# The retention gate's in-projection as pairs of tiles in seven block products, with its token sums made during the value projection

## The chip, the cores and the metric

The kernel runs on one core of one Trainium2 chip. The metric is device time in microseconds. Beside the timed runs there is one profiled execution, from which all rows below come. TensorE (PE) does the matrix products, VectorE (DVE) and ScalarE (ACT) the elementwise work, GpSimd (POOL) and SyncE (SP) mostly issue DMAs, each on a queue of its own that issues in program order.

## The reference

A two-layer decoder trunk on 1024 tokens of width 1024: a retention layer with an MLP, then an attention layer with an MLP, each sub-layer behind an RMS norm with shift and scale from a conditioning vector c. The part in question is the retention layer's in-projection:

```python
def retention_mixer(h, positions, w_in, norm_gain, w_out, gammas):
    proj = h @ w_in                                   # (1024, 1024) @ (1024, 6144)
    q, k, v, g = jnp.split(proj, [qk_w, 2 * qk_w, 2 * qk_w + v_w], axis=-1)
    q, k = rotary(q, positions), rotary(k, positions)
    y = rms_norm(retention(q, k, v, gammas), norm_gain)
    return (jax.nn.silu(g) * y) @ w_out               # g: 2048 columns

ada = c_act @ w_ada[layer] + b_ada[layer]             # shift, scale, gate of each sub-layer
```

The products are in f32. The kernel splits each operand in a high part (rounded) and a low part (the rest) and adds three products, high x high, high x low and low x high.

## The kernel before

Everything is held with features on the partitions and tokens in the free dimension. `h_hi` and `h_lo` hold the normed input (8 tiles of 128 features by 1024 tokens), `xT` the residual stream. Weights come in pairs of tiles: SP loads 256 columns (1 MB) into a slot of `w_raw` (`load_pair`), ACT rounds them into `w_hi` (`prep`, L916), VectorE makes `w_lo` (L1361), TensorE uses them. There are two slots, and SP's next load into one waits for `lo_done`.

The retention in-projection has three stages, each four trips of two pairs: q and k (with rotary), v (tokens as output rows, `v_unit`, L2209 to L2213), and the gate g (`in_body` and `in_unit`, L2077 to L2083). In the gate stage each unit is one tile of 128 columns for 1024 tokens: 8 steps of k, two halves of the tokens, three products, 48 matmuls of 128x512. ACT applies silu while it evacuates (`evac`, L966), POOL spills the tile to `g_s` in DRAM (`spill`, L714).

Beside these stages the modulation is made: for every chunk of 1024 columns of `w_ada` (or `kv_w_ada`) SP loads 8 tiles of 512 KB into two buffers `ada_raw` in turn (`ada_load`, L544), VectorE multiplies each by c and adds it up (`ada_tile`, L1374 and L1377), TensorE sums over the partitions (`ada_sums`, 16 small matmuls, L2153) and VectorE adds the bias (`ada_columns`, L1385). SP's `body` issues one load of weights and then four of the modulation, again and again, and each modulation load waits for the tile two before it. In the gate stage these tiles are all that VectorE does beside `w_lo`.

The first MLP's in-projection already uses seven block products: per pair of tiles, `in_products` (L2420 to L2422) computes seven products of 12 matmuls into three banks. Its weight sums (`in_sums`, L1736 to L1741), splits (`in_low`, L1746) and adds (`add_c22` at L1753 and others) are VectorE's, the copies out of the banks (`keep`) ACT's. Before the seventh product TensorE waits for `add_c22`, which has to read the bank first. No modulation tiles are made in that stage.

After the gate stage the first retention head starts (`ret_head(0)`) on q, k and v that POOL loads back: the first halves (`rq_first`, `rk_first`, `rv_first`) during the gate stage, the rest behind it.

Of the kernel before, what the change touches and what calls it, by code (L numbers as in the profile page):

```python
# [21 lines left out]
ALU = mybir.AluOpType  # L22
# [22 lines left out]
W_QK, W_V, W_G = 0, 8, 16  # L45
W_RET = 24
W_MLP0 = 32
W_FK, W_FV = 36, 40
W_FQ, W_OG = 44, 48
W_FOX = 52  # L50
W_MLP1 = 56


A_QK, A_V, A_G, A_MLP0 = 8, 24, 56, 72
A_FK, A_FF, A_FV, A_FQ, A_OG, A_MLP1, A_OUT = 76, 84, 85, 101, 109, 117, 121
# [10 lines left out]
E_QK, E_V, E_G, E_FK, E_FV, E_FQ, E_OG = 16, 80, 80, 144, 176, 176, 208  # L66
T_V, T_FK, T_FV, T_FQ = 16, 144, 144, 208
# [30 lines left out]
def build(nc, x, vec_a, vec_b, forget_bias, positions, w_ada, kv_w_ada, w_mlp_in, w_mlp_out, ret_w_in,  # L98
          ret_w_out, kv_w, fox_w_in, fox_w_out, ret_decay, out):
    with ExitStack() as ctx:  # L100
# [6 lines left out]
        def region(nbytes, *layouts):  # L107

            base, sets = nc.sbuf_base, []
            for layout in layouts:  # L110
# [23 lines left out]
            _, rq_first, rk_first, rv_first), (_, sq_low) = region(  # L134
# [5 lines left out]
            [("above_ret", [P, 4, S], F32), ("rq_first", [P, 2, HALF], F32), ("rk_first", [P, 2, HALF], F32),  # L140
             ("rv_first", [P, 4, RET_DV], F32)],
# [60 lines left out]
        ada_ps, ada_ps_v = bank[6], bank[0]  # L202
# [101 lines left out]
        z_last_loaded = sem("z_last_loaded")  # L304
        x_moved = [sem(f"x_moved{i}") for i in range(4)]
# [126 lines left out]
        NQ = 14  # L432

# [17 lines left out]
        def in_batch(q, b):  # L451

            raw = (lambda: raw_part(q, 0, 0, 8), lambda: sum_rows(0, 2), lambda: sum_rows(2, 2),
                   lambda: raw_part(q, 1, 4, 4))[b]()
            first, count, n = ((0, 2, P), (2, 2, HALF), (4, 2, HALF), (6, 1, P))[b]
            return raw, split_part(w_hi, first, count, n), split_part(w_lo, first, count, n)
# [11 lines left out]
        def in_operand(i):  # L468
# [4 lines left out]
            return t_tiles({2: 1, 3: 0, 4: 2, 6: 3}[i])[1:]  # L473
# [4 lines left out]
        def t_split(layer, i, order=FIRST_LO):  # L478

            return layer * 4 * (NQ + 1) + order.index(("t", i)) + 1  # L480

        def in_split(layer, q, b, order=FIRST_LO):

            return layer * 4 * (NQ + 1) + (order.index(("w", b)) + 1 if q == 0 else 4 * q + b + 5)

        def t_summed(layer, n):

            return layer * (4 * NQ + 13) + n

        def in_summed(layer, q, n):  # L490

            return layer * (4 * NQ + 13) + 13 + 4 * q + n

        def in_banks(q):

            return (bank[4], bank[5], bank[6]) if q % 2 == 0 else (bank[0], bank[1], bank[2])

# [21 lines left out]
        def _(sp):  # L519
# [46 lines left out]
            with sp.Fori(0, 3) as i:  # L566
                body(i * 2 + W_QK, [in_pair(ret_w_in, i * 512 + 512 + 256 * j) for j in range(2)],
                     i + 2, w_ada[0], i * 1024 + 2048)
            body(W_V - 2, [half_pair(ret_w_in, j, 2048) for j in range(2)], 5, w_ada[0], 5120)
# [3 lines left out]
            for i, (w_a, col_a) in enumerate([(w_ada[1], 3072), (w_ada[1], 4096), (w_ada[1], 5120), (kv_w_ada, 0)]):  # L573
                body(i * 2 + W_G - 2, [in_pair(ret_w_in, i * 512 + 4096 + 256 * j) for j in range(2)],
                     i + 9, w_a, col_a)
            body(W_G + 6, [out_pair(ret_w_out, 0, j) for j in range(2)], 13, kv_w_ada, 1024)
# [4 lines left out]
            def mlp_loads(base, layer, d_end):  # L581
                for j in range(2):
                    load_pair(base + j, j, in_pair(w_mlp_in[layer], 256 * j))

                def x_quarter(hf, kh):
                    return x_s[4 * kh:4 * kh + 4, :, half(hf)].rearrange("k p n -> p k n")
# [5 lines left out]
                def load_in(q):  # L592
                    if q < 2:
                        sp.wait_ge(lo_done, base + q + 1)
                    else:
                        sp.wait_ge(split_lo_done, in_split(layer, q - 2, 3))
# [24 lines left out]
                sp.wait_ge(split_lo_done, in_split(layer, NQ - 2, 3))  # L621
                load_a(0, A11, (0,))
                sp.wait_ge(split_lo_done, in_split(layer, NQ - 1, 2))
                reload_x(1, 1)
                sp.wait_ge(split_lo_done, in_split(layer, NQ - 1, 3))
                load_a(0, A11, (1,))
                sp.wait_ge(in_full, layer * 7 * NQ + 7 * NQ)
# [61 lines left out]
        def _(pool):  # L689
# [52 lines left out]
            for j in range(4):  # L742
                pool.wait_ge(stage_dma[j], E_G)
            for j in range(2):
                pool.wait_ge(stage_dma[T_SLOT + j], T_FK)

# [10 lines left out]
            for dst, src in ((rk_first[:], qk_s[8:10, :, 0:HALF].rearrange("a p n -> p a n")),  # L757
                             (rq_first[:], qk_s[0:2, :, 0:HALF].rearrange("a p n -> p a n")),
                             (rv_first[:], v_s[0:HALF, 0:RET_DV].rearrange("(b p) n -> p b n", p=P))):
                pool.dma_start(dst, src).then_inc(ret_first_loaded, 16)  # L760
            with pool.Fori(0, 4) as i:
                for j in range(4):
                    spill(j, g_s[bass.ds(i * 4 + j, 1)].rearrange("a p n -> p (a n)"),
                          a_free, i * 4 + (A_G + j + 1))
            pool.wait_ge(a_full, A_MLP0)
# [22 lines left out]
            for j in range(4):  # L788
                pool.wait_ge(stage_dma[j], E_FK)
# [116 lines left out]
        def _(act):  # L906
# [104 lines left out]
            def v_trip(i, w_base, a_base, t_base, stage_free, order, after=None):  # L1011

                prep(i * 2 + (w_base + 1), 1)
                prep(i * 2 + (w_base + 2), 0)
# [8 lines left out]
            with act.Fori(0, 4) as i:  # L1023
# [1664 lines left out]
```

## Time and profile before

| | us |
|---|---|
| median of 3 runs | 2971.44 (2969.31 to 2971.76) |
| profiled execution | 2969.84 |
| its span | 2968.2 |
| PE busy | 2926.6 (99%) |
| DVE busy | 1716.2 (58%) |
| ACT busy | 1018.2 (34%) |
| DMA, mean | 145 GB/s |

All times in rows count from the span's start. A matmul is listed with 389 ns, but matmuls are pipelined, so their pitch is read from the starts. PEclk is the granted TensorE clock as a share of 2.4 GHz.

### The profile page before, as it was taken

To read this page: it belongs to the slowest core of one execution; us is meant where nothing else is said; L and a number is where in the kernel's file an instruction comes from. 1 tells how busy PE (TensorE), PEld (TensorE's weight loads), DVE (VectorE), ACT (ScalarE), POOL (GpSimd) and SP (SyncE) were. 2 spreads that over 40 slices of the span, in tenths; PEclk is the share of its full clock that TensorE was granted. 3 is DMA by queue.
4 is the path that set the end of the run, shared out by engine and by line. 5 is a ranking of instruction groups with operands and counts; after the bars stand their busy time and mean duration, and the time that the engine had idled before them with its cause. 6 is when DMAs were issued, how large, how long until landed. Compare 5 with 4: busy or idle time off the path is not lost.

```text
span 2968.2 us, 33444 instructions
## 1 busy us (share of the span) xinstructions
PE 2926.6 (99%) x13020; PEld 2353.8 (79%) x13020; DVE 1716.2 (58%) x2106; ACT 1018.2 (34%) x1287; POOL 339.3 (11%) x486
## 2 busy tenths in 40 slices
PE   7999999999999999999999999999999999999999
PEld 5788888877777888888888787876766888888887
DVE  6664323345457977676756344245455787768673
ACT  5111122233224433334335435334244433333331
POOL 1000010010002000111111001122120200011110
PEclk8999999999999999999999999999999999999999
DMA  6565555542232444565412323455342344475431
GB/s 235 182 208 186 203 192 194 198 169 65 88 118 71 159 144 155 194 233 179 151 35 89 131 79 123 160 131 119 87 105 72 114 160 151 147 261 192 135 135 57
DMA packets 182630, 431.01 MB, mean 145 GB/s; under 512 B 12849, under 2 KB 74724, under 8 KB 182500
## 3 DMA queue, kind: packets, MB, share of 16 engines
q0 software_dynamic: 61616, 222.34, 22.5%
q1 hardware_dynamic: 120884, 206.88, 20.9%
q8 instruction: 88, 1.44, 0.2%
q14 instruction: 42, 0.34, 0.0%
HBM read 309.90 MB, written 119.14 MB: 145 GB/s over the span
## 4 chain that ended last, share of the span: by engine, by line
PE 91%; DVE 4%; ACT 2%; DMA 1%; issue 1%; POOL 0%; SPq 0%; DVEq 0%; ACTq 0%; POOLq 0%
PE ps L2442 6%; PE ps L2422 6%; PE ps L2444 6%; PE ps L2421 6%; PE ps L2420 6%; PE ps L2440 6%; PE ps L2077 5%; PE ps L2083 5%; PE ps L2080 5%; PE ps L2121 4%; PE ps L2120 4%; PE ps L2117 4%; PE ps L2572 3%; PE ps L2209 3%; PE ps L2213 3%; PE ps L2212 3%
## 5 line engine op out<-in xcount | busy, mean ns | idle before, releaser
L2440 PE MATMUL ps<-z_hi,w_hi 128*128 128x512 f32 x768 | 299.0, 389 | 0.0
L2444 PE MATMUL ps<-z_hi,w_lo 128*128 128x512 f32 x768 | 299.0, 389 | 0.0
L2442 PE MATMUL ps<-z_lo,w_hi 128*128 128x512 f32 x768 | 299.0, 389 | 0.0
L2077 PE MATMUL ps<-h_hi,w_hi 128*128 128x512 f32 x704 | 275.8, 392 | 2.7 <-DVE w_lo L1361 2.2
L2080 PE MATMUL ps<-h_lo,w_hi 128*128 128x512 f32 x704 | 274.6, 390 | 0.0
L1361 DVE TENSOR_TENSOR w_lo<-w_raw,w_hi 128x2048 fp32r<-128x2048 f32 x60 | 137.4, 2290 | 149.8 <-ACT w_hi L916 149.8
L2083 PE MATMUL ps<-h_hi,w_lo 128*128 128x512 f32 x704 | 217.7, 391 | 0.0
L2117 PE MATMUL ps<-z_hi,w_hi 128*128 128x512 f32 x512 | 203.6, 398 | 0.0
L2121 PE MATMUL ps<-z_hi,w_lo 128*128 128x512 f32 x512 | 199.6, 390 | 0.0
L2120 PE MATMUL ps<-z_lo,w_hi 128*128 128x512 f32 x512 | 199.5, 390 | 0.0
L916 ACT ACTIVATE w_hi<-w_raw 128x2048 fp32r<-128x2048 f32 x60 | 114.6, 1910 | 221.5 <-PE ps L2209 116.7
L1377 DVE SCALAR_TENSOR_TENSOR misc<-misc,c_act 128x1024 f32<-128x1024 f32 x84 | 107.9, 1284 | 125.8 <-DMA misc<-w_ada 105.9
L1530 DVE SCALAR_TENSOR_TENSOR xT<-ps,ada,xT 128x512 f32<-128x512 f32 x128 | 93.9, 748 | 147.5 <-PE ps L2121 147.5
L966 ACT ACTIVATE stage<-ps 128x1024 f32<-128x1024 f32 x56 | 57.4, 1026 | 344.8 <-PE ps L2083 274.8
L2422 PE MATMUL ps<-h_hi,w_lo 128*128 128x512 f32 x448 | 174.4, 389 | 0.0
L2421 PE MATMUL ps<-h_lo,w_hi 128*128 128x512 f32 x448 | 174.4, 389 | 0.0
L2420 PE MATMUL ps<-h_hi,w_hi 128*128 128x512 f32 x448 | 174.4, 389 | 0.0
L2440 PEld LDWEIGHTS ps<-z_hi,w_hi 128*128 128x128 f32 x768 | 144.2, 188 | 29.9
L2442 PEld LDWEIGHTS ps<-z_lo,w_hi 128*128 128x128 f32 x768 | 144.2, 188 | 29.8
L2444 PEld LDWEIGHTS ps<-z_hi,w_lo 128*128 128x128 f32 x768 | 144.2, 188 | 29.8
L2077 PEld LDWEIGHTS ps<-h_hi,w_hi 128*128 128x128 f32 x704 | 132.7, 188 | 31.0 <-DVE w_lo L1361 3.5
L2083 PEld LDWEIGHTS ps<-h_hi,w_lo 128*128 128x128 f32 x704 | 132.6, 188 | 27.7
(345 smaller groups left out, 6360.6 us busy)
## 6 DMA issues: line engine op xcount, KB each, us to landing
t_s<-misc POOLq DMA_DIRECT2D x28, 1792.0 KB, 6.9
misc<-t_s POOLq DMA_DIRECT2D x98, 512.0 KB, 4.1
misc<-w_ada SPq DMA_DIRECT2D x80, 512.0 KB, 5.1
w_raw<-w_mlp_in SPq DMA_DIRECT2D x32, 1024.0 KB, 5.5
w_raw<-ret_w_in SPq DMA_DIRECT2D x24, 1024.0 KB, 7.7
a_bufs<-w_mlp_out SPq DMA_DIRECT2D x12, 1024.0 KB, 22.7
a_bufs<-w_mlp_out SPq DMA_DIRECT2D x12, 768.0 KB, 6.0
qk_s<-stage POOLq DMA_DIRECT2D x16, 512.0 KB, 4.0
```

The costliest lines, as they stand in the source:

```text
L2077: m = MM(outs[hf], hi, b_hi[:, k, cols], start=first, stop=False)
L2080: MM(outs[hf], hi, b_lo[:, k, cols], start=False, stop=False)
L2083: m = MM(outs[hf], lo, b_hi[:, k, cols], start=False, stop=last)
L2117: mm = MM(out_bank, hi, z_hi[:, k, half(hf)], start=k == 0, stop=False)
L2120: MM(out_bank, hi, z_lo[:, k, half(hf)], start=False, stop=False)
L2121: mm = MM(out_bank, lo, z_hi[:, k, half(hf)], start=False, stop=k == 3)
L2420: MM(out, hi, b_hi[:, k, :], start=k == 0 and i in (0, 1, 3), stop=False, skip_group_check=True)
L2421: MM(out, hi, b_lo[:, k, :], start=False, stop=False, skip_group_check=True)
L2422: mm = MM(out, lo, b_hi[:, k, :], start=False, stop=k == 3, skip_group_check=True)
L2440: MM(bank[at + m], hi, ring_b(z_hi, slot)[:, cols], start=first and i not in (2, 4, 5), stop=False, skip_group_check=True)
L2442: MM(bank[at + m], hi, ring_b(z_lo, slot)[:, cols], start=False, stop=False, skip_group_check=True)
L2444: mm = MM(bank[at + m], lo, ring_b(z_hi, slot)[:, cols], start=False, stop=last, skip_group_check=True)
```

## The change

The gate stage uses the seven products too, for 8 pairs of tiles, 84 matmuls a pair in place of 96. The former function inside the MLP becomes one for three phases (`ph` 0 is the gate, 1 and 2 the MLPs), with counters offset by the pairs before. What is added, and where:

- SP spills the four quarters of `xT` to scratch behind the last q/k loads, and loads them back when the last pair's adds are done. In between `xT` holds four sums of the tokens' blocks.
- VectorE makes these sums (`gate_t_sums`, ten operations of 128x2048) behind the modulation tiles of the first three value trips; ACT and VectorE split them before and after the fourth. The order of VectorE's work in the gate stage is written out by hand, below.
- SP loads a gate pair into `w_raw` when the pair two before it has been split, and four modulation tiles behind it.
- ACT copies three partial products a pair, applies silu to the finished tiles in place, and loads silu's table once. POOL spills two tiles a pair, from two slots instead of four.
- The first loads for retention move behind the seventh pair's spills and wait for products of the eighth pair.

```diff
 # SP
+            for n in range(4):
+                sp.dma_start(x_quarter(n // 2, n % 2), xT[quarter(n // 2, n % 2)]).then_inc(x_moved[n], 16)
+            def load_gate(q):
+                if q < 2:
+                    sp.wait_ge(lo_done, W_V + 7 + q)
+                else:
+                    sp.wait_ge(split_lo_done, in_split(0, q - 2, 3))
+                sp.dma_start(dst, in_pair(ret_w_in, 4096 + 256 * q)).then_inc(in_loaded[q % 2], 16)
+            for i, (w_a, col_a) in enumerate([... five chunks, the first is chunk 9 ...]):
+                for j in range(2):
+                    if i < 4:
+                        load_gate(2 * i + j)
+                    else:
+                        sp.wait_ge(split_lo_done, in_split(0, NG - 2 + j, 3))
+                        load_pair(W_RET + j, j, out_pair(ret_w_out, 0, j), first=True)
+                    for k in range(4 * j, 4 * j + 4):
+                        ada_load(i + 9, k, w_a, col_a)
+            sp.wait_ge(c_added, added(0, NG - 1, 3))
+            for n in range(4):
+                sp.dma_start(xT[quarter(n // 2, n % 2)], x_quarter(n // 2, n % 2)).then_inc(x_moved[n], 16)
 # ACT
+            for q in range(NG):
+                if q:
+                    gate_out(q - 1)          # silu of the fourth tile, out of the bank
+                    gate_high(q, 3)          # waits for the seventh product of q - 1
+                    gate_silu(q - 1)         # in place, two operations; POOL spills after them
+                gate_keep(q, 0)
+                if q + 1 < NG:
+                    gate_high(q + 1, 0)
+                gate_keep(q, 1)
+                gate_keep(q, 2)
+                if q + 1 < NG:
+                    gate_high(q + 1, 1)
+                    gate_high(q + 1, 2)
 # VectorE
+            def gate_low(q, b):
+                raw, hi, lo = in_batch(q, b, gate_sum_rows)
+                dve.wait_ge(split_hi_done, in_split(0, q, b))
+                TT(lo, raw, hi.bitcast(F32), ALU.subtract).then_inc(split_lo_done, 1)
+            v_trip(3)
+            gate_sums(0)
+            gate_t_low(2)
+            gate_t_low(1)
+            gate_low(0, 0)
+            gate_low(0, 1)
+            ada_columns(9, ada_ps_v)
+            gate_low(0, 2)
+            gate_t_low(3)
+            gate_low(0, 3)
+            for q in range(NG):
+                chunk = 10 + q // 2
+                if q:
+                    gate_low(q, 3)
+                    if q % 2 == 0:
+                        ada_columns(chunk - 1, ada_ps_g)
+                for k in range(4 * (q % 2), 4 * (q % 2) + 2):
+                    ada_tile(chunk, k)
+                if q + 1 < NG:
+                    gate_sums(q + 1)
+                    gate_low(q + 1, 0)
+                for k in range(4 * (q % 2) + 2, 4 * (q % 2) + 4):
+                    ada_tile(chunk, k)
+                if q + 1 < NG:
+                    gate_low(q + 1, 1)
+                for n in range(3):
+                    gate_add(q, n)
+                if q + 1 < NG:
+                    gate_low(q + 1, 2)
+                else:
+                    prep(W_RET, 0)
+            ada_columns(13, ada_ps_g)
 # TensorE
+            for q in range(NG):
+                in_products(0, q, ((A_V + 25, A_V + 26, A_V + 27), (A_MLP0, 0, 0)), gate_t_tiles, gate_banks)
+                if q % 2:
+                    ada_sums(10 + q // 2, ada_ps=ada_ps_g)
 # inside in_products, as in the MLP before
                 for i in range(7):
                     if i in (0, 2, 4, 6):
+                        pe.wait_ge(split_lo_done, in_split(ph, q, i // 2))
                     if i == 6:
+                        pe.wait_ge(c_added, added(ph, q, 1))
```

## Rows read from the trace of the kernel before

**Rows 1.** The page: busy time of TensorE, and the chain that ended last.
```profile
PE 2926.6 (99%) x13020; PEld 2353.8 (79%) x13020; DVE 1716.2 (58%) x2106; ACT 1018.2 (34%) x1287; POOL 339.3 (11%) x486
...
PE 91%; DVE 4%; ACT 2%; DMA 1%; issue 1%; POOL 0%; SPq 0%; DVEq 0%; ACTq 0%; POOLq 0%
```

**Rows 2.** Windows (busy us per engine, PEclk, DMA share, GB/s): value, gate, MLP in-products.
```profile
242.10:423.70 181.60, 181.59 (x832) 151.47 (x833) 64.01 (x50) 33.44 (x39) 11.79 (x17) 1.00 0.55 188
423.70:605.20 181.50, 181.50 (x835) 151.45 (x834) 57.10 (x43) 42.80 (x34) 12.66 (x22) 1.00 0.56 193
...
988.65:1255.20 266.55, 266.55 (x1177) 220.82 (x1176) 195.85 (x250) 91.39 (x118) 17.93 (x20) 1.00 0.47 165
```

**Rows 3.** Timeline of TensorE (start, us): end of the gate stage, edges of the in-products.
```profile
605.03 0.53 PE L2295 MATMUL ps<-ident,rk_first 128*128 128x128 f32 x3
...
988.65 0.39 PE L2420 MATMUL ps<-h_hi,w_hi 128*128 128x512 f32 x1
...
1255.21 0.39 PE L2440 MATMUL ps<-z_hi,w_hi 128*128 128x512 f32 x1
```

**Rows 4.** Groups of TensorE in the gate stage, the first of three.
```profile
L2077 PE MATMUL ps<-h_hi,w_hi 128*128 128x512 f32 x256 | 100.0, 391 | 0.0
```

**Rows 5.** Timeline of VectorE: a split of weights, and two modulation tiles.
```profile
403.89 2.29 DVE L1361 TENSOR_TENSOR w_lo<-w_raw,w_hi 128x2048 fp32r<-128x2048 f32 x1
...
586.84 2.60 DVE L1377 SCALAR_TENSOR_TENSOR misc<-misc,c_act 128x1024 f32<-128x1024 f32 x2
```

**Rows 6.** Waits of VectorE in the value and gate stages (us in total, times, longest).
```profile
DVE misc L1377 <- DMA misc<-w_ada: 68.4, 30, 6.5
```

**Rows 7.** Timeline of VectorE in the MLP's fourth pair: split, sums, split, add.
```profile
1047.12 0.69 DVE L1746 TENSOR_TENSOR w_lo<-w_raw,w_hi 128x512 fp32r<-128x512 f32 x1 [1.55 <-ACT w_hi L1123]
...
1052.73 0.68 DVE L1736 TENSOR_TENSOR xT<-w_raw 128x512 f32<-128x512 f32 x1
...
1055.26 1.22 DVE L1746 TENSOR_TENSOR w_lo<-w_raw,w_hi 128x1024 fp32r<-128x1024 f32 x1
...
1059.57 0.69 DVE L1753 TENSOR_TENSOR misc<-ps,low_tiles 128x512 f32<-128x512 f32 x1
```

**Rows 8.** Timeline of SP's queue: two bursts of weights and modulation tiles.
```profile
406.21 0.38 SPq L529 DMA_DIRECT2D w_raw<-ret_w_in  x1
406.63 0.58 SPq L544 DMA_DIRECT2D misc<-w_ada  x1
...
407.25 0.43 SPq L544 DMA_DIRECT2D misc<-w_ada  x1
...
541.58 0.38 SPq L529 DMA_DIRECT2D w_raw<-ret_w_out  x1
...
544.09 0.33 SPq L544 DMA_DIRECT2D misc<-kv_w_ada  x1
```

**Rows 9.** DMA issues (KB, us to landing): the tiles issued at 406.63, 407.25, 544.09.
```profile
misc<-w_ada SPq DMA_DIRECT2D x1, 512.0 KB, 7.6
...
misc<-w_ada SPq DMA_DIRECT2D x1, 512.0 KB, 9.1
...
misc<-kv_w_ada SPq DMA_DIRECT2D x1, 512.0 KB, 5.3
```

**Rows 10.** Timeline of TensorE: two starts after idle time (in brackets).
```profile
1678.37 0.80 PE L2209 MATMUL ps<-w_hi,h_hi 128*128 128x512 f32 x1 [2.30 <-ACT misc L1269]
...
1786.18 0.50 PE L2077 MATMUL ps<-h_hi,w_hi 128*128 128x512 f32 x1 [2.18 <-DVE w_lo L1361]
```

**Rows 11.** Windows behind these two starts; the third figure from the end is PEclk.
```profile
1678.30:1681.50 3.20, 3.13 (x8) 2.51 (x9) 1.22 (x1) 1.93 (x2) 0.72 (x2) 0.51 0.96 378
1787.30:1790.50 3.20, 3.20 (x9) 2.51 (x8) 0.00 (x0) 2.19 (x2) 1.64 (x4) 0.50 0.89 249
```

**Rows 12.** Timeline of ACT at the start and end of the gate stage.
```profile
425.82 1.92 ACT L916 ACTIVATE w_hi<-w_raw 128x2048 fp32r<-128x2048 f32 x1
...
604.57 1.28 ACT L909 ACT_TABLE_LOAD   x1
```

More of the change, by code:

```diff
@@ new lines, in gate_high @@
+            def gate_high(q, b):
+                raw, hi, _ = in_batch(q, b, gate_sum_rows)
+                if q == 0 and b < 2:
+                    act.wait_ge(w_begun, W_V + 8)
+                elif q == 0:
+                    act.wait_ge(a_full, A_MLP0)
+                else:
+                    act.wait_ge(in_full, full(0, q - 1, (2, 4, 6, 7)[b]))
+                if b in (0, 3):
+                    act.wait_ge(in_loaded[q % 2], raw_loaded(0, q))
+                else:
+                    act.wait_ge(in_sum_done, in_summed(0, q, (3, 4)[b - 1]))
+                nc.scalar.activation(hi, raw, ACT.Copy).then_inc(split_hi_done, 1)
@@ new lines, in before_gates, with gate_keep @@
+            def before_gates():
+                for i in (2, 1):
+                    gate_t_high(i)
+                gate_high(0, 0)
+                gate_high(0, 1)
+            with act.Fori(0, 3) as i:
+                v_trip(i, W_V, A_V, T_V, (rot_done, 8), V_ORDER)
+            gate_t_high(0)
+            v_trip(3, W_V, A_V, T_V, (rot_done, 8), V_ORDER, before=before_gates)
+            def gate_keep(q, n):
+                i, at, reader = ((0, 0, 2), (2, 0, 3), (3, 2, 1))[n]
+                act.wait_ge(in_full, full(0, q, i + 1))
+                if q:
+                    act.wait_ge(c_added, added(0, q - 1, reader))
+                elif n == 2:
+                    act.wait_ge(split_lo_done, t_split(0, 3))
+                nc.scalar.activation(g_kept[n], gate_banks(q)[at], ACT.Copy).then_inc(p_copied, 1)
@@ new lines, in gate_out, with gate_silu @@
+            def gate_out(q):
+                act.wait_ge(in_full, full(0, q, 7))
+                for j in range(2):
+                    act.wait_ge(stage_dma[T_SLOT + j], T_G + 16 * q)
+                nc.scalar.activation(g_tiles[:, 2, :], gate_banks(q)[0], ACT.Silu).then_inc(p_copied, 1)
+            def gate_silu(q):
+                act.wait_ge(c_added, added(0, q, 3))
+                nc.scalar.activation(g_tiles[:, 0:2, :], g_tiles[:, 0:2, :], ACT.Silu).then_inc(g_done, 1)
+                nc.scalar.activation(g_tiles[:, 3, :], g_tiles[:, 3, :], ACT.Silu).then_inc(g_done, 1)
@@ new lines, in _ @@
+            nc.scalar.preload_act_table_set("silu_and_others")
+            gate_high(0, 2)
+            gate_t_high(3)
+            gate_high(0, 3)
+            for q in range(NG):
[11 more added lines that the diff above has]
+                    gate_high(q + 1, 2)
+                else:
+                    act.wait_ge(in_full, full(0, q, 4))
+                    prep(W_RET, 0, first=True)
@@ L1026, in _ @@
+            gate_out(NG - 1)
+            gate_silu(NG - 1)
             log_and_exp()
@@ L1509, in _, with gate_t_sums @@
             step.end(2)
-            with dve.Fori(0, 4) as i:
+            def gate_t_sums(i):
+                out = xT[(quarter(0, 0), quarter(1, 1), quarter(1, 0), quarter(0, 1))[i]]
+                plus = ((1, 0), (1, 1), (1, 1), (0, 1))[i]
+                minus = (quarter(0, 0), quarter(0, 0), quarter(1, 0), quarter(1, 1))[i]
+                at = quarter(*plus)
+                done = t_summed(0, (0, 6, 3, 8)[i])
+                if i in (1, 3):
+                    dve.wait_ge(in_sum_done, done)
+                first = xT[minus] if i in (1, 3) else h_hi[minus].bitcast(F32)
+                TT(out, h_hi[at].bitcast(F32), first, ALU.subtract).then_inc(in_sum_done, 1)
+                dve.wait_ge(in_sum_done, done + 1)
+                TT(out, out, h_lo[at].bitcast(F32), ALU.add).then_inc(in_sum_done, 1)
+                if i in (0, 2):
+                    dve.wait_ge(in_sum_done, done + 2)
+                    TT(out, out, h_lo[minus].bitcast(F32), ALU.subtract).then_inc(in_sum_done, 1)
@@ L1652, in ret_head @@
                     add_squares(1, v)
+                if first:
+                    for n in range(4):
+                        dve.wait_ge(x_moved[n], 32)
                 add(0)
```

321 lines of the change are left out of this document (196 added, 125 removed).

## The prediction

> **What bounds the kernel now.** I read the page first: TensorE is busy 99% of the span and 91% of the chain that ended last [rows 1]. Then one window per stage: in the value projection, in the gate projection and in the in-products of the first MLP, TensorE is busy for the whole window while VectorE is busy for 64.0, 57.1 and 195.9 us [rows 2]. So the kernel is bound by the number of matmuls. The timeline gives their pitch: the 14 pairs of the MLP's in-products, which already use the seven products, run from 988.65 to 1255.21 us, 1176 matmuls in 266.56 us or 0.2267 us each, 19.04 us a pair (the 389 ns of one overlap) [rows 3]. The gate projection runs from 423.70 to 605.03, 181.3 us [rows 2, 3]: 768 matmuls (three lines of 256, the first in [rows 4]) are 174.1 us, so the four column sums of the modulation (16 small matmuls each) are 1.8 us each. Whatever is late in the gate stage is paid in full, since nothing else covers TensorE.
>
> **Removed.** Eight pairs of tiles took 96 matmuls each; seven products of 12 are 84. 8 x 12 x 0.2267 = 21.8 us go. If TensorE never waited, the stage would take 159.5 us. That is the most the change can bring.
>
> **Added on VectorE in the value projection.** Ten sums of 128x2048, 2.3 us each as the w_lo line of that size [rows 5], three t_low and four weight sums: some 35 us beside 64.0 busy of 181.6 [rows 2]. They stand behind each trip's prep; the trace releases w_raw at 406.18, 17.5 us before TensorE needs that pair at 423.70 [rows 2, 5], and the longest run of sums is 4 x 2.3 = 9.2 us. I take nothing; without that cover each trip could lose at most the 9.2 us, so 0 to 9 for the whole. The spill of xT (4 transfers of 1 MB) stands on SP behind the last QK loads, where VectorE isn't near the path; taken at nothing, with at most the length of the transfer (10 us) in front of loads that have 17 us of room. It can't gain.
>
> **The steady pair of the gate stage.** This is where I find the price. In the MLP, VectorE does the same sums, splits and adds and waits for no load on this path. In the gate stage it also makes four modulation tiles a pair, and the order is what counts. On SP, load_gate(q + 2) waits until gate_low(q, 3) has freed w_raw, and the four modulation tiles that VectorE uses in pair q are issued behind that same load. On VectorE, two of these tiles are the first thing after gate_low(q, 3), ahead of gate_sums(q + 1), gate_low(q + 1, 0), two more tiles, gate_low(q + 1, 1), and then gate_add(q, 0), for which TensorE waits before the seventh product. In the kernel before, the same loads were already issued a half trip ahead; VectorE waited for them too (68.4 us in 30 waits over both stages [rows 6]), but nobody waited for VectorE. From the end E of the previous pair:
> - gate_low(q, 3) ends: in the MLP the fourth pair starts at 988.65 + 3 x 19.04 = 1045.77, the same split ends at 1047.12 + 0.69 = 1047.8: 2.0 us [rows 3, 7].
> - The burst of 1 MB weights and two tiles, with a spill on POOL's queue beside it: released at 406.18, the second tile issued at 407.25 and landed 9.1 later, at 416.35: 10.2 us [rows 5, 8, 9]. The first lands at 406.63 + 7.6 = 414.2. Two g spills instead of one v spill will stand beside it here. Bounds: without a spill the second tile lands at 544.09 + 5.3 = 549.4, 7.8 after the weights' issue, in which it had itself waited a little for VectorE [rows 8, 9], so I put the low end at 7.3; with another 512 KB at the rate of such a burst, 11.5. I take 10.2, the nearest row.
> - VectorE from there: second tile 1.3 (two take 2.60), gate_sums 2.5 (1052.73 to 1055.26), gate_low 1.2, two tiles 2.6, gate_low 1.2, the add 0.7: 9.5 us [rows 5, 7].
> - The seventh product, 12 matmuls: 2.7.
> Sum: 2.0 + 10.2 + 9.5 + 2.7 = 24.4 us a pair, where the kernel before takes 181.3 / 8 = 22.7 and an unhindered one 19.04. TensorE stands idle for 2.0 + 10.2 + 9.5 - 16.3 (six products) = 5.4 us before the seventh product, 3.6 where a column sum (now hidden) stood in the pair.
>
> **The clock.** At 1678.37 and 1786.18 TensorE had been idle for 2.30 and 2.18 us [rows 10], and within about a microsecond it ran at the lower level, granted 0.51 and 0.50 of 2.4 GHz, so 1.2 GHz [rows 11]. The windows of 3.2 us hold 8 matmuls where 14 would have started: 6 x 0.2267 = 1.4 us a fall. Gaps of 3.6 to 5.4 us are longer than both, and the slow stretch falls on the seventh product, which the loop waits for. I add 1.4 a pair: 25.8. Bounds 0 (the fall is over before the gap is) and 2.4 (the seventh product wholly at the lower level). The Trainium skill ("TensorE: Matmul & The Clock Gate", Why this matters for your kernels) warns only of idle gaps a little longer than these two; by that rule the gaps of 2.2 us should have cost nothing, which the trace contradicts, and for the gaps forecast here, all longer than those, rule and rows give the same sum.
>
> **First and last pair.** At 423.70 ACT evacuates and loads a table until 425.8, then rounds 1024 and 2048 columns (1.92 for the 2048 [rows 12]) until about 428.7, and VectorE's splits of the fourth token sum (2.3) and of the last weights (0.7) end at about 431.6, 7.9 after the start. The burst without spills is 7.8, VectorE 9.5, the product 2.7, the clock 1.4: 29.3. In the last pair VectorE has no sums and splits, but waits for the loads of its third and fourth tile (issued when the first and second are used, 4 to 5 us each): 2.0 + 16.0 + 2.7 + 1.4 + 2.1 for tile and add = 24.2. The stage: 29.3 + 6 x 25.8 + 24.2 + 1.8 (last column sum) = 210.1 us, 28.8 more than before.
>
> **Into retention.** ACT now finishes with two silus after its last evacuation, about 1.3 us later than the single one, ahead of the table load (604.57, 1.28) and of the keys [rows 12]; the product of the keys waits, 1.0. POOL's second loads go out 1 us later and beside 4 MB of xT coming back: 1.0, bounds 0 and 4. Together 2.0. The first loads now go in the last pair, 24 us long, which covers them. Nothing after that is touched: the MLPs only count differently.
>
> **Sum.** 28.8 + 2.0 = 30.8. The profiled execution had a span of 2968.2 us and took 2969.84 in all, so 3000.6; the median of the three runs shown is 1.6 above it: 3002 us, 1.0% slower.
>
> The Trainium skill ("DMA: Bandwidth & Descriptors", Anatomy of one DMA) gives a fit of 2.0 us fixed plus the bytes at 436 GB/s. As an estimate from it, 2 MB in one burst would be there after 6.8 us; the trace's 7.8 and 10.2 are longer, and by the fit the sum would be about 3.4 us less in each of seven pairs, some 2978. The same page's rules for kernel authors ask for an early issue and a late wait, and the change does the reverse with the modulation's tiles.
>
> **Rivals.**
> 1. Exposed, but the clock holds (or falls inside the gap): 3002 - 8 x 1.4 = 2991. For it: only two gaps in the trace show the fall. Against: both did. 0.17.
> 2. Short bursts: second tile at 7.3. The steady pair is 21.5, the last 20.4, the first 27.9: 179.1 with the column sum, about 2971 with the 2.0 behind; with the falls of the clock 2982. For it: bursts without spills nearly do that [rows 8, 9]. Against: the spills of g are due just then. 0.15.
> 3. The loads are hidden after all, and TensorE never waits: -21.8 + 2.0, 2952. It decides if the two first tiles land within 4.8 us of the release, or if some load is ahead in a way that I overlook in the order of SP's queue. For it: VectorE has 14 us of work in a pair of 19, and the MLP runs the same scheme without a gap [rows 2, 3]. Against: the first tile alone needed 8.0 [rows 5, 8, 9]. 0.18.
> 4. My forecast, with the fall in every pair: 0.50. Its own range is 2992 to 3013 (burst 9.3 to 11.5).
>
> A change within 0.2% (6 us) can't be told from none here; call that "same". Cases 4 and 1 are slower, case 2 is split between slower (0.06) and same (0.08, with 0.01 faster), case 3 is faster. Faster 0.19, same 0.08, slower 0.73. The range reaches from the middle of case 2 to the high end of case 4: 2972 to 3013.
>
> **What would show it.** In the profile of the changed kernel: 672 matmuls of seven products at a pitch of 0.2267 between gaps; a wait of TensorE on VectorE's add ahead of the seventh product in every pair, about 5 and 3.5 us in turns and some 9 in the first; ahead of it a wait of VectorE for the modulation's tile of about 8 us right after gate_low(q, 3); PEclk under 1 in the slices of the gate stage; that stage about 210 us. If the waits on the add are absent, step two of the pair is wrong and case 3 holds. If they are there and short, the landing was mis-sized. If the value projection takes more than 181.6 us, the sums or the spill of xT weren't free.

## The result and the profile after

| | us |
|---|---|
| before, median of 4 runs beside it | 2971.6 (2969.31 to 2972.93) |
| changed kernel, median of 4 runs | 3011.38 (3007.2 to 3017.87) |
| ratio | 1.0143, 95% interval 1.0131 to 1.0156 |
| profiled execution of the changed kernel, its span | 3017.87, 3016.3 |

The change costs 1.4%, where 1.0% was forecast: the median is 39.8 us above that of before, the forecast said 30.8. The profiled execution was the slowest of the four and stands 48.0 us above the one shown of before (3017.87 less 2969.84), so 6.5 us of what follows is this execution's own.

The page, against [rows 1]; then the line of the first of the three matmuls that in-products issue (the gate's and the MLPs' are one line now), with its idle time:

```profile
PE 2926.3 (97%) x12924; PEld 2347.2 (78%) x12924; DVE 1796.1 (60%) x2200; ACT 1044.7 (35%) x1340; POOL 338.9 (11%) x486
...
PE 85%; DVE 5%; DMA 5%; ACT 2%; issue 2%; SPq 0%; POOL 0%; DVEq 0%; ACTq 0%; POOLq 0%
...
L2514 PE MATMUL ps<-h_hi,w_hi 128*128 128x512 f32 x576 | 231.7, 402 | 44.6 <-DVE stage L1699 36.7
```

96 matmuls are gone (12924 for 13020), yet TensorE is busy as long as before: much of what the products saved was lost to a slower clock. And the chain that ended last runs 10% through VectorE and DMA, where it was 5%. The windows of the two projections and of the first MLP's in-products, against [rows 2]:

```profile
245.30:428.45 183.15, 183.15 (x832) 152.52 (x833) 95.75 (x68) 38.96 (x43) 11.79 (x17) 0.99 0.52 177
428.45:650.90 222.45, 177.40 (x741) 143.96 (x740) 105.66 (x121) 63.04 (x82) 11.95 (x21) 0.89 0.50 167
1037.24:1303.80 266.56, 266.56 (x1178) 220.79 (x1176) 196.23 (x250) 91.38 (x118) 17.94 (x20) 1.00 0.47 165
```

The MLP is unchanged to the hundredth. The value projection took VectorE's 31.7 us of sums without a wait; its 1.5 us more are one fall of the clock at its start, and six of the eight experiments below have 181.6 there. The loss is in the gate stage: 45.0 us in which TensorE isn't busy, and a mean granted clock of 0.89. What TensorE waited for in the gate stage and at the start of retention:

```profile
PE ps L2514 <- DVE stage L1699: 36.7, 7, 6.6
PE ps L2514 <- DVE w_lo L1691: 7.9, 1, 7.9
```

L1699 is the add (`gate_add`), and its 7 waits are one for each pair but the first. There the profile names a split (L1691), but the splits that this product needs had ended at 436.36, 17 us before; the first add ended at 453.49, 0.11 us before TensorE started. So TensorE waited for the add in all eight pairs. The first pair's add on VectorE and the product behind it on TensorE:

```profile
452.81 0.68 DVE L1699 TENSOR_TENSOR stage<-ps,xT 128x512 f32<-128x512 f32 x1
```

```profile
453.60 0.77 PE L2514 MATMUL ps<-h_hi,w_hi 128*128 128x512 f32 x1 [7.89 <-DVE w_lo L1691]
```

One steady pair on VectorE (timeline: start, us, line, tile, idle time before and its releaser):

```profile
459.39 0.69 DVE L1691 TENSOR_TENSOR w_lo<-w_raw,w_hi 128x512 fp32r<-128x512 f32 x1 [3.57 <-ACT w_hi L1115]
469.05 1.28 DVE L1519 SCALAR_TENSOR_TENSOR misc<-misc,c_act 128x1024 f32<-128x1024 f32 x1 [8.97 <-DMA misc<-w_ada]
471.41 1.28 DVE L1519 SCALAR_TENSOR_TENSOR misc<-misc,c_act 128x1024 f32<-128x1024 f32 x1 [1.07 <-DMA misc<-w_ada]
...
480.35 0.68 DVE L1699 TENSOR_TENSOR stage<-ps,xT 128x512 f32<-128x512 f32 x1
```

The split `gate_low(1, 3)` ends at 460.08, SP's queue issues the weights and then the tiles (first fence), POOL's spills go out in the same microsecond (second), and TensorE starts the seventh product after 6.63 us of idle time, in the next pair after 4.14 (third):

```profile
460.11 0.38 SPq L629 DMA_DIRECT2D w_raw<-ret_w_in  x1
460.54 12.51 SPq L589 DMA_DIRECT2D misc<-w_ada  x4
```

```profile
460.91 1.08 POOL L777 DMA_DIRECT2D g_s<-stage  x2 [28.57 <-ACT stage L1145]
```

```profile
481.18 0.76 PE L2514 MATMUL ps<-h_hi,w_hi 128*128 128x512 f32 x1 [6.63 <-DVE stage L1699]
...
507.91 0.47 PE L2514 MATMUL ps<-h_hi,w_hi 128*128 128x512 f32 x1 [4.14 <-DVE stage L1699]
```

VectorE's own work from the second tile (471.41) to the add's end (481.03) is 9.6 us, as forecast. The clock, in windows from inside the gap of 6.63, behind it, and behind the gap of a later pair:

```profile
477.50:481.18 3.68, 0.00 (x1) 0.03 (x1) 3.22 (x5) 0.00 (x0) 0.00 (x0) 0.51 0.01 2
481.18:484.40 3.22, 3.22 (x8) 2.54 (x9) 2.18 (x3) 0.00 (x0) 0.00 (x0) 0.50 0.00 0
...
588.72:592.12 3.40, 3.40 (x8) 2.72 (x9) 2.18 (x3) 0.00 (x0) 0.00 (x0) 0.50 0.00 0
```

It falls in the gap and is still at 1.2 GHz for 3.2 us of the product in one pair, for 4.9 us, nearly the whole product, in another (588.72 to 593.6).

### The profile page after: what moved, and what is told of

Its sections match the earlier page's. It is cut to its first block, busy times and chain, and to the rows that moved or that the text cites. A ratio compares the mean times of both kernels' runs of the same rounds, so it can differ in the third digit from the quotient of the medians.

```text
span 3016.3 us, 33307 instructions
## 1 busy us (share of the span) xinstructions
PE 2926.3 (97%) x12924; PEld 2347.2 (78%) x12924; DVE 1796.1 (60%) x2200; ACT 1044.7 (35%) x1340; POOL 338.9 (11%) x486
## 4 chain that ended last, share of the span: by engine, by line
PE 85%; DVE 5%; DMA 5%; ACT 2%; issue 2%; SPq 0%; POOL 0%; DVEq 0%; ACTq 0%; POOLq 0%
PE ps L2514 6%; PE ps L2515 6%; PE ps L2516 6%; PE ps L2676 6%; PE ps L2678 6%; PE ps L2674 6%; PE ps L2352 4%; PE ps L2351 4%; PE ps L2348 4%; PE ps L2806 3%; PE ps L2308 3%; PE ps L2314 3%; PE ps L2311 3%; PE ps L2440 3%; PE ps L2443 3%; PE ps L2444 3%
## 5 line engine op out<-in xcount | busy, mean ns | idle before, releaser
L2514 PE MATMUL ps<-h_hi,w_hi 128*128 128x512 f32 x576 | 231.7, 402 | 44.6 <-DVE stage L1699 36.7
L2515 PE MATMUL ps<-h_lo,w_hi 128*128 128x512 f32 x576 | 229.8, 399 | 0.0
L2516 PE MATMUL ps<-h_hi,w_lo 128*128 128x512 f32 x576 | 229.6, 399 | 0.0
L1503 DVE TENSOR_TENSOR w_lo<-w_raw,w_hi 128x2048 fp32r<-128x2048 f32 x52 | 119.0, 2289 | 115.2 <-ACT w_hi L981 115.2
L2308 PE MATMUL ps<-h_hi,w_hi 128*128 128x512 f32 x448 | 175.6, 392 | 2.7 <-DVE w_lo L1503 2.2
L2311 PE MATMUL ps<-h_lo,w_hi 128*128 128x512 f32 x448 | 174.9, 390 | 0.0
L981 ACT ACTIVATE w_hi<-w_raw 128x2048 fp32r<-128x2048 f32 x52 | 99.3, 1909 | 203.3 <-PE ps L2440 98.8
L2514 PEld LDWEIGHTS ps<-h_hi,w_hi 128*128 128x128 f32 x576 | 112.0, 194 | 71.1 <-DVE w_lo L1691 40.8
L2440 PE MATMUL ps<-w_hi,h_hi 128*128 128x512 f32 x384 | 151.5, 395 | 2.9 <-ACT misc L1411 2.3
L2806 PE MATMUL ps<-misc,fv 128*128 128x512 f32 (+1 forms) x360 | 151.6, 503 | 0.9 <-ACT misc L1447 0.9
L2201 DVE CUSTOM_DVE_ANT_0 ps<-ps,row_mask 128x1024 f32<-128x1024 f32 (+3 forms) x120 | 90.8, 767 | 101.9 <-PE ps L2763 100.6
```

Source lines behind the costliest of these rows:

```text
L2308: m = MM(outs[hf], hi, b_hi[:, k, cols], start=first, stop=False)
L2311: MM(outs[hf], hi, b_lo[:, k, cols], start=False, stop=False)
L2514: MM(out, hi, b_hi[:, k, :], start=k == 0 and i in (0, 1, 3), stop=False, skip_group_check=True)
L2515: MM(out, hi, b_lo[:, k, :], start=False, stop=False, skip_group_check=True)
L2516: mm = MM(out, lo, b_hi[:, k, :], start=False, stop=k == 3, skip_group_check=True)
L2806: MM(bank[6 + hf][:, HALF - w:HALF], keys, probs[:, probs_slot(e), 0:w], start=b == 0, stop=n in (HF0 - 1, NF - 1)).then_inc(pv_done, 1)
```

## The experiments

All times are ratios to the kernel before on the same chip. "Release" is SP's issue of the weights behind gate_low(q, 3) (where a kernel puts the tiles first, that of the weights all the same); a steady pair is the mean distance of the six releases from the second to the eighth. The gate stage is taken from the first gate product to the first score of retention, 181.8 us before.

| kernel | median us | ratio [95%] | steady pair | gate stage |
|---|---|---|---|---|
| changed | 3011.38 | 1.0143 [1.0131, 1.0156] | 27.15 | 222.5 |
| tiles ahead | 2958.09 | 0.9964 [0.9949, 0.9978] | 20.24 | 167.4 |
| sums first | 2979.27 | 1.0031 [1.0017, 1.0046] | 22.87 | 188.2 |
| fill | 2998.78 | 1.0098 [1.0081, 1.0115] | 25.36 | 209.7 |
| small spills | 2985.13 | 1.0055 [1.0039, 1.0072] | 23.44 | 198.7 |
| weights last | 2987.45 | 1.0061 [1.0043, 1.0080] | 23.68 | 193.5 |
| ahead, late reload | 2955.48 | 0.9950 [0.9937, 0.9964] | 20.23 | 166.7 |
| and late table | 2954.76 | 0.9945 [0.9932, 0.9959] | 20.29 | 165.2 |
| and own count | 2950.11 | 0.9944 [0.9930, 0.9958] | 20.26 | 163.4 |

**Tiles ahead.** The test of the whole mechanism: two loads are issued earlier, nothing else.

```diff
                 for j in range(2):
+                    for k in range(4 * j, 4 * j + 2):
+                        ada_load(i + 9, k, w_a, col_a)
                     if i < 4:
                         load_gate(2 * i + j)
 ...
-                    for k in range(4 * j, 4 * j + 4):
+                    for k in range(4 * j + 2, 4 * j + 4):
```

> SP issues the first two modulation tiles of each pair before it waits for the split that frees the weights' slot, instead of behind that load; all else as in the changed kernel. Theory (the seventh product waits because VectorE stands at two tiles whose loads were issued only after gate_low(q, 3)): these two are there at once, the third and fourth land some 8 us after their issue, the add ends about 16 us into the pair, as the sixth product does. Waits of TensorE on the add under 1.5 us or gone, gate stage 160 to 170 us instead of 222, in all 2950 to 2962. Rival A (VectorE's added sums and splits are too much for a pair of 19 us, whenever the tiles come): the waits stay near 4 to 6 us and the time within 10 us of 3011.

Measured: 2958.09, inside the expectation. TensorE's waits in the gate stage, and VectorE in one pair, where the first two tiles follow gate_low(q, 3) without a gap:

```profile
PE ps L2555 <- DMA rv_first<-v_s: 2.4, 1, 2.4
PE ps L2516 <- DVE w_lo L1693: 1.7, 1, 1.7
PE ps L2516 <- DVE stage L1701: 1.1, 2, 0.6
```

```profile
467.02 0.69 DVE L1693 TENSOR_TENSOR w_lo<-w_raw,w_hi 128x512 fp32r<-128x512 f32 x1 [1.99 <-ACT w_hi L1117]
...
467.71 0.75 DVE L1518 TENSOR_SCALAR misc<-misc,c_act 128x1024 f32<-128x1024 f32 x1
468.56 1.28 DVE L1521 SCALAR_TENSOR_TENSOR misc<-misc,c_act 128x1024 f32<-128x1024 f32 x1
...
481.32 0.69 DVE L1701 TENSOR_TENSOR stage<-ps,xT 128x512 f32<-128x512 f32 x1
```

Eight waits of 44.6 us in all shrink to three of 2.8 (the one named w_lo is again the first pair's wait for its add), and 53 us go. Most of the rest is the clock: it didn't fall in any of the eight pairs, where in the changed kernel 32 us of its lower level lay on the products, 16 us of work. The new wait for rv_first and the fall beside it take some of this back. VectorE does exactly the same work, so rival A (too much of it) falls. With the loads in time the seven products are faster than the plain ones, by 0.36%.

**Sums first.** The other way to take the landing off the path: VectorE's order.

```diff
-                for k in range(4 * (q % 2), 4 * (q % 2) + 2):
-                    ada_tile(chunk, k)
                 if q + 1 < NG:
                     gate_sums(q + 1)
                     gate_low(q + 1, 0)
-                for k in range(4 * (q % 2) + 2, 4 * (q % 2) + 4):
+                for k in range(4 * (q % 2), 4 * (q % 2) + 2):
                     ada_tile(chunk, k)
 ...             # second split, the three adds, as before
                 if q + 1 < NG:
                     gate_low(q + 1, 2)
-                else:
+                for k in range(4 * (q % 2) + 2, 4 * (q % 2) + 4):
+                    ada_tile(chunk, k)
+                if q + 1 == NG:
                     prep(W_RET, 0)
```

> VectorE's order alone is changed: sums and first split of the next pair stand right behind gate_low(q, 3), then two modulation tiles, second split, the adds, third split, and the last two tiles; SP's order is that of the changed kernel. Theory: the 3.7 us of sums and split go beside the landing, and two tiles (2.6 us and their wait) leave the path to the add, which then ends about 11.2 + 1.3 + 1.2 + 0.7 = 14.4 after the release, 16.4 into the pair, where the sixth product ends at 16.3. The wait before the seventh product is under 1 us; the column sums of the modulation, which need all four tiles, wait about 2 us in every second pair. Gate stage about 170 us, in all 2955 to 2968. Rival A (too much work on VectorE): within 10 us of 3011.

Measured: 2979.27, 11 us above the expectation's end. The first half nearly held: the add's waits are 3.6 us in all and 1.5 in the first pair, the longest 1.7 where under 1 was expected. The rest:

```profile
PE ps L2384 <- DVE misc L1519: 11.7, 4, 6.2
PE ps L2514 <- DVE stage L1699: 3.6, 3, 1.7
PE ps L2514 <- DVE w_lo L1691: 1.5, 1, 1.5
```

The column sums (L2384) stood for the last two tiles in every second pair, three times for 1.8 us, as expected, and for 6.2 in the last. What the expectation left out is the clock, which fell again behind each of these waits (24 us at the lower level in this trace's gate stage, 48 in the changed kernel's). The wait moved with the loads; of the orders tried, only issuing them earlier removes it.

**Fill.** The clock by itself.

```diff
+                    if ph == 0 and i == 6:
+                        if q == 0:
+                            pe.wait_ge(a_free, A_MLP0)
+                        n_fill = (24 if q % 2 or q == 0 else 16)
+                        f_hi = in_operand(5, tiles)[0]
+                        for f in range(n_fill):
+                            MM(bank[7], f_hi[:, (f + 1) % 4, 0:P], f_hi[:, f % 4, :], ...)
                     if i == 6:
                         pe.wait_ge(c_added, added(ph, q, 1))
```

> TensorE multiplies 24 times (16 in pairs 2, 4 and 6) into a bank that is free, just before it waits for the add of the seventh product; nothing else changes, the products computed are the same. It sizes the clock: the gaps are filled (24 x 0.2267 = 5.4 us, 16 = 3.6) and the wait that is left is 0.5 to 2.5 us. Theory (each gap makes the clock fall and costs 1.4 to 1.7 us of the products behind it): the granted clock stays at 1.0 in most pairs and the time goes down by some 10 to 13 us to about 3000. Rival B (the fall is over within the gap, or the remaining short gap triggers it as well): no change, 3007 to 3015.

Measured: 1.0098 for 1.0143, by these ratios 13.4 us less, though TensorE does 168 matmuls more. The whole stage at a clock of 0.99 (one fall in it, in the first pair, where 2.6 us were still empty):

```profile
425.23:634.89 209.66, 202.15 (x910) 165.62 (x908) 105.72 (x121) 63.09 (x82) 11.99 (x21) 0.99 0.52 174
```

The landings stayed what they were (second tile 10.5 to 11.5 us behind the release), so the 1.8 us that a steady pair lost are the clock's part. Rival B falls.

**Small spills.** What stands beside the burst.

```diff
-                    spill(T_SLOT + u, g_s[2 * q + u], g_done, 2 * q + u + 1)
+                    wait_run(g_done, 2 * q + u + 1)
+                    pool.dma_start(g_s[2 * q + u][:, 0:16], stage[:, T_SLOT + u, 0:16])...
```

> POOL spills only 16 of 1024 columns of each finished gate tile, and retention reads q and k in the gates' place: two transfers of 512 KB a pair go, which stood beside the burst of weights and modulation tiles. It sizes the burst. Theory (the spills lengthen the landing from 7.8 to about 11.2 us): the second tile lands about 8 us after the release, each steady pair is about 3 us shorter, 20 to 25 us in all, time 2986 to 2992. Rival C (the 2 MB of the burst on SP's queue alone take that long): less than 6 us, 3005 to 3012.

Measured: 2985.13, 26 us less and 1 us under the expectation. This kernel leaves out all but a 64th of each gate tile and reads q and k in their place, so it is there for its time alone. The same pair as above, release at 454.84:

```profile
454.12 0.69 DVE L1692 TENSOR_TENSOR w_lo<-w_raw,w_hi 128x512 fp32r<-128x512 f32 x1 [3.71 <-ACT w_hi L1116]
461.23 1.28 DVE L1520 SCALAR_TENSOR_TENSOR misc<-misc,c_act 128x1024 f32<-128x1024 f32 x1 [6.42 <-DMA misc<-w_ada]
463.50 1.28 DVE L1520 SCALAR_TENSOR_TENSOR misc<-misc,c_act 128x1024 f32<-128x1024 f32 x1 [0.99 <-DMA misc<-w_ada]
```

The second tile is used 8.7 us after the release, where the spills made it 11.3 in the same pair. Rival C falls: the spills are worth 3.7 us a pair, with the falls of the clock that shorter gaps save (27 us at the lower level in this trace's stage).

**Weights last.** The place inside the burst.

```diff
                 for j in range(2):
+                    gate_free(2 * i + j)          # the wait that load_gate had
+                    for k in range(4 * j, 4 * j + 2):
+                        ada_load(i + 9, k, w_a, col_a)
                     if i < 4:
                         load_gate(2 * i + j)      # without its wait
                     else:
-                        sp.wait_ge(split_lo_done, in_split(0, NG - 2 + j, 3))
                         load_pair(W_RET + j, j, out_pair(ret_w_out, 0, j), first=True)
-                    for k in range(4 * j, 4 * j + 4):
+                    for k in range(4 * j + 2, 4 * j + 4):
                         ada_load(i + 9, k, w_a, col_a)
```

> SP waits for the split as in the changed kernel, but then issues the two modulation tiles first and the 1 MB of weights behind them. It tells apart what the place within the burst is worth from what the wait ahead of the burst costs. Theory (the tiles land late because 1 MB stands before them on the same queue): the second tile lands 6 to 7 us after the release instead of 11.2; the third and fourth, now behind the weights, make VectorE wait 1 to 2 us; the wait before the seventh product is 2 to 4 us, a steady pair takes 22.5 to 23.5 us instead of 27.15, in all 2972 to 2985. Rival D (the transfers share the DMA engines, so that all of a burst lands together whatever the order): the second tile still lands after about 11 us and the time stays at 3005 to 3012.

Measured: 2982.21, 2987.45 and 2988.66 (a fourth run took 6607.28 and is left out), ratio 1.0061, 2 us above the expectation's end. Tiles issued at 455.09 and 455.5 were used at 459.08 and 461.53; the third, behind the weights, made VectorE wait again:

```profile
459.08 1.28 DVE L1523 SCALAR_TENSOR_TENSOR misc<-misc,c_act 128x1024 f32<-128x1024 f32 x1 [4.02 <-DMA misc<-w_ada]
461.53 1.28 DVE L1523 SCALAR_TENSOR_TENSOR misc<-misc,c_act 128x1024 f32<-128x1024 f32 x1 [1.17 <-DMA misc<-w_ada]
...
469.17 1.29 DVE L1523 SCALAR_TENSOR_TENSOR misc<-misc,c_act 128x1024 f32<-128x1024 f32 x1 [2.68 <-DMA misc<-w_ada]
```

The second tile is used 6.4 us after the first one's issue, where in the changed kernel it was 11.3 after the weights' issue: what is issued first on a queue does land first, rival D falls. But the gap stays at up to 4.6 us (19.2 in seven waits, and 5.2 in the first pair): a little under half of what "tiles ahead" gained was the order in the burst (1.0143 to 1.0061, then to 0.9964), and the wait ahead of it is the rest.

**Late reload, late table, own count.** Three small steps on top of "tiles ahead".

```diff
+            sp.wait_ge(ret_second_loaded, 48)         # late reload: ahead of the four reloads of xT
 ...
-            nc.scalar.preload_act_table_set("silu_and_others")
             gate_high(0, 2)
             gate_t_high(3)
             gate_high(0, 3)
+            nc.scalar.preload_act_table_set("silu_and_others")   # late table
 ...
-                pool.dma_start(dst, src).then_inc(ret_first_loaded, 16)
+                pool.dma_start(dst, src).then_inc(first_v_loaded if n == 4 else ret_first_loaded, 16)
 # own count, on TensorE: the keys wait for 80 in place of 96, the state product for rv_first
```

> The kernel with the two tiles ahead (median 2958.1), and SP issues the four reloads of xT only when retention's second loads have landed. Theory (the 4 MB of xT stand beside rv_first, which landed after 7.9 us and kept TensorE 2.4 us): rv_first lands 5 to 6 us after its issue, the wait shrinks to 0 to 0.5 us, in all 1.5 to 2.5 us less, about 2956. xT is back well before it is first added to, 40 us behind. Rival E (rv_first is slow because of POOL's own loads and the weights of W_RET): no change, 2957 to 2959; or the later reload delays the weights of the second head: 1 to 5 us more.

Measured: 2955.48. The wait for rv_first shrank from 2.4 to 1.8 us, its landing from 7.9 to 7.5: xT's reload had little to do with it, and rival E was nearer, though which of its two causes holds wasn't tried. The 2.6 us between the medians, or 1.4 in a thousand between ratios with intervals of 1.4 either side, can't be told from none.

> As the kernel before it in this list, and ACT loads silu's table after its last split of the first gate pair instead of before its first. Theory (in the first pair TensorE waited 1.7 us for gate_low(0, 3), the end of a chain ACT to VectorE to ACT that begins with the table load of 1.28 us): that wait goes from 1.7 to about 0.4 us and 1.3 us in all, with 1.5 more where the clock had fallen for it; about 2954.5. Rival F (VectorE was late by itself, or the load is now ahead of the first copy out of a bank and delays the third product): no change from the kernel before it in the list.

Measured: 2954.76. The first pair's wait went from 1.7 us to 0.5, where 0.4 was expected, but the step in the time, 0.7 us, is below what can be measured. The expectation had the place of the wait wrong: gate_low(0, 3) ends 11 us before that product starts, and what TensorE waits for is the add. The split is the start of VectorE's chain to it, and with the split 1.4 us earlier the add came 1.3 us earlier (17.6 us into the stage for 18.9).

> As the kernel with the late table (median 2954.8), and rv_first has a count of its own: the transpositions and scores of the first retention head start when rk_first and rq_first are there, and only the state product waits for rv_first. Theory (TensorE stood 1.6 us for rv_first, which is needed 2 to 4 us later than the keys, and the clock fell for that wait, which made the products of the first head some 1.3 to 2.5 us longer): the wait on DMA vanishes or falls under 0.5 us, the clock does not fall at 592, in all 2 to 4 us less, 2951 to 2953. Rival G (the keys, through ACT, are then what the state product waits for, 1 us at ACT's end, and this gap makes the clock fall as well): under 1 us less, 2954 to 2955.

Measured: 2950.11, ratio 0.9944, the same as without it (0.9945), so the time doesn't decide. The trace does: the wait for the load is gone, 0.9 us for the keys stand in its place, and the clock didn't fall. The window 586 to 600 us with the late table, then with the own count, whose stage ends 5.6 us sooner (its trace has no fall at all between 151 and 1659 us):

```profile
586.00:600.00 14.00, 12.42 (x57) 9.06 (x56) 4.16 (x8) 7.17 (x9) 4.03 (x6) 0.88 0.93 309
```

```profile
586.00:600.00 14.00, 13.10 (x63) 9.98 (x62) 5.21 (x6) 5.61 (x8) 3.75 (x6) 1.00 0.95 320
```

This version has the lowest time, 0.56% below the kernel before. Its gain over "tiles ahead" is 2.0 in a thousand, with an interval of about 1.4 either side on each of the two ratios, so even the sum of the three steps is not clear of the noise; the gate stage of the traces, 163.4 for 167.4 us, is one execution each.

## Why the prediction was right in kind and short in size

**Right.** The forecast's case 4 came about: exposed, with a fall in every pair. Removed: 96 matmuls, as counted. The value projection and xT's spill cost nothing [rows 2], the order of loads on SP and of tiles on VectorE set the path, VectorE's work behind the second tile is 9.6 us for the 9.5 forecast, TensorE waited for the add in all eight pairs, and the first pair came as worked out: release 7.9 us into it, seventh product 17.2 after the release for 17.3. Cases 1 to 3 fell: the clock didn't hold, bursts weren't short, and the loads weren't hidden. The rule in the Trainium skill ("DMA: Bandwidth & Descriptors", Rules for kernel authors) that a DMA be issued early and waited for late is what "tiles ahead" follows; here it was worth 53 us. The fit that the prediction quotes from the Trainium skill ("DMA: Bandwidth & Descriptors", Anatomy of one DMA) would have put the sum at 2978, farther from the measured time; it is given there for one transfer issued from GpSimd, and this burst is three on SP's queue.

That the clock would fall in every pair was forecast on thin grounds. The two rows for it [rows 10] have gaps of 2.2 and 2.3 us, and in the ten traces here the clock fell behind these two places in 8 and in 6 of the ten, so "both did" was partly chance. Behind gaps of 3.6 us and more, as they came about here, it fell 16 times in 16 (all ten traces, from 160 us on).

**Short.** The path was right and its sizes were not. The step that failed is the steady pair, forecast at 25.8 us and measured at 27.15: its landing ("I take 10.2") was 10.9, and its clock ("I add 1.4 a pair") some 2.0. The last pair, whose 16.0 us to the fourth tile were 18.9, comes on top. The stage was to take 210.1 us and took 222.0 (428.45 to 650.45). Its terms:

- **The landing.** "Two g spills instead of one v spill will stand beside it" was seen, but the value taken was the row with one spill, 10.2, not the high end of 11.5. In the six steady pairs the second tile was used 11.3, 10.9, 10.8, 10.7, 11.4 and 10.4 us after the release, 10.9 in the mean: 0.7 a pair. "Small spills" shows the cause.
- **The clock.** 1.4 a fall was read from windows of 3.2 us where the engine had stopped for 2.2 and 2.3 us [rows 10, 11]; the clock was down for 3.4 us each time, of which 3.4 and 3.1 fell on work. Here the clock was down for 6.8 us in six of the eight pairs and for 3.4 in two, and what counts is how much of that falls on the product: 3.2 to 5.2 us, at most the whole product. From the start of the seventh product to the next release 6.8 us passed, in the mean of the six pairs, for 2.0 + 2.7 + 1.4 = 6.1: some 0.6 a pair. "Fill" gives the clock's part from the other side, 1.8 a pair in place of 1.4.
- **The last pair.** 16.0 us was to pass from the release to the fourth tile; it was 18.9 (623.03 to 641.91, below). The fourth tile, issued at 634.94, landed after 7.0 us where 4 to 5 were forecast, and retention's first loads went out on POOL's queue just then. No run moves these loads alone, so that they are the cause is read from the trace and not tested. The prediction had moved them into this pair, "24 us long, which covers them", and asked only whether they were late themselves, not what they did to the tiles. With 0.6 for the clock, 3.4.

```profile
636.62 1.28 DVE L1519 SCALAR_TENSOR_TENSOR misc<-misc,c_act 128x1024 f32<-128x1024 f32 x1 [1.71 <-DMA misc<-kv_w_ada]
641.91 1.28 DVE L1519 SCALAR_TENSOR_TENSOR misc<-misc,c_act 128x1024 f32<-128x1024 f32 x1 [4.01 <-DMA misc<-kv_w_ada]
```

```profile
634.61 0.72 POOL L828 DMA_DIRECT2D rk_first<-qk_s  x1 [9.77 <-DMA g_s<-stage]
635.32 0.73 POOL L828 DMA_DIRECT2D rq_first<-qk_s  x1
636.05 0.75 POOL L828 DMA_DIRECT2D rv_first<-v_s  x1
```

Together 6 x 1.35 + 3.4 + 0.4 (first pair's clock) = 11.9, the difference. The rest of this execution's excess of 17.3 over the forecast: 0.6 more than the 2.0 behind the gate stage (where a score waits 1.9 for the second half of v and the state product 0.9 for the keys), and 4.8 ahead of it, which are a start of the q/k projection 2.0 us later and two falls of the clock, at 153.3 and at 245.4. These come and go between executions: of the other nine traces four have the first fall, two have the second, and the start varies from 48.0 to 51.9 us. The median run is 6.5 us shorter than this one; it has no trace, so which terms are smaller in it isn't known. The forecast's own range (case 4) moved the burst alone: the clock's stated upper bound, 2.4 for 1.4 a pair, would have added 8 us to its high end, and its low end of 2992 doesn't follow from a burst of 9.3, which is 0.9 less in eight pairs and gives 2995.

What stays open: the price of xT's return. From the first score to the first MLP product the changed kernel takes 386.3 us, "tiles ahead" 385.7, "own count" 384.2 and before 383.2; how much of this is the reload's isn't known. "Late reload", which issues it later, has 385.6, so its place there isn't what costs. It wasn't left out alone, since without it the sums would stand where the residual is read.

## What to carry to other kernels

When an engine gets new work between two waits, ask of every load that it uses not "is there time for it in a pair" but "what must happen before it is issued": here two small loads were queued behind a wait that the same engine's last instruction released, and this turned a gain of 0.4% into a loss of 1.4%. Size a burst by all that is in flight beside it, on every queue, and count what a load moved to a new place does to its neighbours there. And price an idle gap of TensorE with its clock: about 1.8 us on top of each gap here, which cheap matmuls into a free bank can buy back where the gap itself can't be closed.

## What the runs showed of the hardware

- Whether the clock falls, and for how long, doesn't follow the gap alone. Behind full products of 128x512 a gap of 2.18 or 2.19 us at one place had a fall in 8 of ten traces and one of 2.30 or 2.31 at another in 6 of ten. In "weights last" a gap of 3.09 us had none and one of 2.17 none; in "small spills" one of 2.98 had one; all 16 gaps from 3.60 us up had one (ten traces, from 160 us on). In the changed kernel it was down for 3.4 us after gaps of 3.85 and 4.14, and for 6.8 after one of 3.60 and all longer ones. The Trainium skill ("TensorE: Matmul & The Clock Gate", HAM oscillation) puts the danger at longer gaps than 2.2 and 2.3 us; the gaps from 3.60 us up agree with it, the 14 falls in 20 behind the two short ones don't.
- The waits under 2 us that had a fall beside them (not all had) stand beside the sixteen column sums, matmuls of 128x1 that take 1.8 us together. In "tiles ahead", "late reload" and "late table" the sums come first and then a wait of 2.36, 1.76 and 1.58 us for rv_first; the clock was down for 6.8, 6.8 and 3.4 us, and in the first two the eight score products took 2.77 us where they take 1.48 at full clock. In "sums first" the sums follow waits of 1.8 us, three falls in three. In "weights last" a wait of 0.55 us behind them was enough. Elsewhere no gap under 2 us had one, from 160 us of the span on.
- When TensorE was kept busy by products that nobody reads, the clock stayed up in seven of eight pairs, though up to 1.1 us of each gap were still empty.
- Three of the ten traces (that of the changed kernel is one) have a fall of 3.4 us right at the start of the value projection, where TensorE waits 0.55 to 0.58 us in all of them, directly behind column sums. It costs about 1.5 us and comes and goes between executions of kernels that are alike up to there.
- Transfers on different queues slow each other (the second tile is used 7.6 to 9.0 us behind the release without spills beside it, 10.4 to 11.4 with, in steady pairs), while within one queue what is issued first lands first (6.4 against 11.3).
